# Scoring two neighbouring blocks of queries in one go, with one pool of four score and turn banks

## The reference

```python
# first block: 8 heads of 64; causal, ALiBi slope (with 2 blocks of 256 and top-1 selection,
# every earlier key is attended)
s = q.k * 64**-0.5 - slope * (tq - ks);  s = where(ks <= tq, s, -1e30)
out = softmax(s) @ v
# second block, layer 0: differential attention, 8 heads, two score matrices per head, all 512 keys
pr = softmax(s);  a = pr[:, 0] - lam * pr[:, 1];  o = rms_norm(a @ v) * 0.8
# second block, layer 1: sliding window, 16 query heads on 4 key/value heads, |i-j| <= 128, and a
# sink logit per head, which takes part in the softmax but has no value
mask = abs(kpos - qpos) <= 128
m = max(max(s), sink);  e = exp(s - m);  pr = e / (sum(e) + exp(sink - m))
```

## Time and profile before

| | us |
|---|---|
| median of 3 runs (lowest, highest) | 1973.62 (1973.46, 1975.21) |
| span of the profiled execution | 1972.9 |
| first attention, about | 36 to 166 |
| differential attention, about | 730 to 955 |
| sliding attention, about | 1385 to 1545 |

### The profile page before, as it was taken

One profiled execution on the slowest core, in us unless ns is written; L12 is line 12 of the kernel. 1 busy time (PEld: TensorE's weight loads), 2 busy tenths in 40 slices (PEclk: granted clock), 3 DMA queues, 4 the chain that ended last, 5 costly groups with the idle time before them and its releaser, 6 DMA issues.

```text
span 1972.9 us, 25163 instructions
## 1 busy us (share of the span) xinstructions
PE 1940.0 (98%) x9232; PEld 1590.0 (81%) x9232; DVE 1188.4 (60%) x1952; ACT 924.4 (47%) x1740; POOL 1109.2 (56%) x842
## 2 busy tenths in 40 slices
PE   8999999999999999999999999999999999999997
PEld 6877888888888877777888888888777888888886
DVE  6773325353433488877675646856688675746855
ACT  5653336533333366555453433445477543443443
POOL 5345544454444456454576665755785576666662
PEclk9999999999999999999999999999999999999998
DMA  4122233232232321111322222223110323222321
GB/s 160 65 70 96 89 114 128 95 104 102 97 111 94 111 98 68 45 65 54 128 103 100 97 96 97 97 90 109 65 54 33 128 97 107 97 86 96 107 93 57
DMA packets 52106, 182.72 MB, mean 93 GB/s; under 512 B 5776, under 2 KB 6160, under 8 KB 51984
## 3 DMA queue, kind: packets, MB, share of 16 engines
q1 hardware_dynamic: 51984, 181.12, 26.4%
HBM read 174.80 MB, written 6.29 MB: 92 GB/s over the span
## 4 chain that ended last, share of the span: by engine, by line
PE 92%; DVE 5%; ACT 1%; issue 1%; DMA 0%; POOL 0%; SPq 0%; DVEq 0%; ACTq 0%; POOLq 0%
PE b L393 28%; PE b L395 28%; PE b L394 28%; PE b L415 2%; PE b L407 1%; PE b L448 1%; PE b L439 1%; PE b L438 1%; DVE sm L574 1%; PE b L408 1%; PE b L409 1%; DVE ra L621 1%; DVE fa L586 0%; PE b L426 0%; DVE ra L483 0%
## 5 line engine op out<-in xcount | busy, mean ns | idle before, releaser
L239 POOL TENSOR_TENSOR ra<-raw,ra 128x512 fp32r<-128x512 f32 x632 | 883.2, 1405 | 771.7 <-ACT ra L283 770.0
L393 PE MATMUL b<-ra 128*128 128x512 f32 x2528 | 1000.7, 396 | 15.9 <-POOL ra L239 9.4
L395 PE MATMUL b<-ra 128*128 128x512 f32 x2528 | 985.9, 390 | 0.0
L394 PE MATMUL b<-ra 128*128 128x512 f32 x2528 | 985.2, 390 | 0.0
L283 ACT ACTIVATE ra<-raw 128x512 fp32r<-128x512 f32 x632 | 392.8, 628 | 531.9 <-PE b L395 526.4
L393 PEld LDWEIGHTS b<-ra 128*128 128x128 f32 x2528 | 475.5, 188 | 121.2 <-issue 15.2
L395 PEld LDWEIGHTS b<-ra 128*128 128x128 f32 x2528 | 475.0, 188 | 101.0
L394 PEld LDWEIGHTS b<-ra 128*128 128x128 f32 x2528 | 475.7, 188 | 93.3
L737 DVE TENSOR_TENSOR h<-b,h 128x512 f32<-128x512 f32 x136 | 91.8, 683 | 61.4 <-PE b L395 60.6
L628 DVE TENSOR_TENSOR tmp<-b,rb 128x512 f32<-128x512 f32 x62 | 42.4, 689 | 100.2 <-PE b L395 100.0
L621 DVE TENSOR_TENSOR ra<-b,ra 128x512 fp32r<-128x512 f32 (+4 forms) x166 | 91.9, 567 | 17.6 <-ACT ra L334 14.8
(11 more groups left out here) (276 smaller groups left out, 1900.4 us busy)
## 6 DMA issues: line engine op xcount, KB each, us to landing
raw<-in_f_g SPq DMA_DIRECT2D x40, 512.0 KB, 3.5
raw<-in_f_v SPq DMA_DIRECT2D x40, 512.0 KB, 3.5
raw<-in_f_d SPq DMA_DIRECT2D x40, 512.0 KB, 3.5
raw<-in_w_up SPq DMA_DIRECT2D x32, 512.0 KB, 3.5
raw<-in_w_down SPq DMA_DIRECT2D x32, 512.0 KB, 3.5
raw<-in_p_g SPq DMA_DIRECT2D x16, 512.0 KB, 3.5
raw<-in_w_gp SPq DMA_DIRECT2D x8, 512.0 KB, 3.4
raw<-in_w_ga SPq DMA_DIRECT2D x8, 512.0 KB, 3.4
```

The costliest lines, as they stand in the source:

```text
L239: e.tensor_tensor(wl, src, wh.bitcast(F), ALU.subtract).then_inc(*w_low.mark(n))
L393: e.matmul(ps, wh[:, c:c + 128], xh, start=start, stop=False)
L394: e.matmul(ps, wh[:, c:c + 128], xl, start=False, stop=False)
L395: last = e.matmul(ps, wl[:, c:c + 128], xh, start=False, stop=stop)
```

## The change

Two neighbouring blocks of queries, i and i + 1, are scored in one step of the planner. That step issues four tiles (12 matmuls) where there were two steps of two tiles, and it needs four free banks and four free probability buffers (in the differential attention two buffers of each kind). The two pairs of banks become one pool of four, QB, from which scores and turns take the bank that comes free first. With the banks no longer tied to heads, the sink column is written for every tile, after its score and before its `mask_min`: 64 copies. The planner's duration of a score step changes with it.

```diff
-            return (3 * (0.012 + a[1] / 2400.0) + 0.2) if a[4] == 0 else 0.04
+            return (3 * (0.012 + a[1] / 2400.0) + (0.35 if a[10] else 0.0)) if a[4] == 0 else 0.02
...
-    sbk = [2, 3]
-    tbk = [4, 5]
+    QB = [2, 3, 4, 5]
...
+    def picked(n):
+        ready = sorted((b for b in QB if bank_free[b] is not None), key=lambda b: sc.time_of(bank_free[b]))
+        return ready[:n] if len(ready) >= n else None
+    def pick(l):
+        ready = [b for b in l if bank_free[b] is not None]
+        return min(ready, key=lambda b: sc.time_of(bank_free[b])) if ready else None
...
@@ turns_of, and in the same way v_tile @@
-                b = rot(tbk)
+                b = pick(QB)
...
@@ attention_pairs, soft @@
+            if sinks:
+                made += sinks(t, b, score)
             n = row("mask_min", x["p"][:, 0:wide], banks[b][:, c0(i):c0(i) + wide], mk, slope(t), nm, score,
                     (*x["free"], *made))
             v = done("ve", "soft_v", n)
             bank_free[b] = (v,)
-            if i == 3 and sinks and t + 2 < 2 * npairs:
-                sinks(t + 2, b)
...
@@ attention_pairs, scores; together is 2 in both calls @@
-            for i in range(4):
+            for i2 in range(0, 4, together):
                 def need():
-                    if len(PB.free) < 2 or None in (bank_free[sbk[0]], bank_free[sbk[1]]):
+                    if len(PB.free) < 2 * together or picked(2 * together) is None:
                         return None
...
-                yield 8 * p + 2 * i, "pe", need
+                yield 8 * p + 2 * i2, "pe", need
+                steps = []
+                for i in range(i2, i2 + together):
+                    for t in (2 * p, 2 * p + 1):
+                        b = pick(QB)
+                        n = row("score", b, nk, c0(i), (qh, ql), rw, (kh, kl), i, lo, bank_free[b], (*qt, *kt_), i == i2)
+                        steps.append((t, i, b, done("pe", "score", n)))
+                for x in steps:
+                    launch(soft(*x))
...
@@ attention_diff, scores @@
-                    if not PB.free or not T.free or None in (bank_free[sbk[0]], bank_free[sbk[1]]):
+                    if len(PB.free) < 2 or len(T.free) < 2 or None in [bank_free[b] for b in QB]:
...
-        def sinks(t, b):
-            sunk[t] = (done("ve", "soft_v", row("sink_column", b, t, bank_free[b])),)
-            bank_free[b] = sunk[t]
+        def sinks(t, b, score):
+            return (done("ve", "soft_v", row("sink_column", b, t, (score,))),)
```

More of the change, by code:

```diff
@@ L401, in tensor_program @@
         elif kind == "score":
-            b, nk, c0, (qh, ql), row, (kh, kl), i, lo, free, ready = a
+            b, nk, c0, (qh, ql), row, (kh, kl), i, lo, free, ready, _ = a
             for t in free + ready:
@@ L1258, in need @@
                 def need():
-                    if (t, i) not in p_done or bank_free[tbk[0]] is None or (t and (t - 1, i // 2) not in used):
+                    if (t, i) not in p_done or pick(QB) is None or (t and (t - 1, i // 2) not in used):
                         return None
-                    return (p_done[(t, i)], *bank_free[tbk[0]])
+                    return (p_done[(t, i)], *bank_free[pick(QB)])
                 yield rank0(t) + per * i, "pe", need
@@ L1304, in heads, with attention_pairs @@
         launch(products_of(0))
-    def attention_pairs(npairs, Q, KT, VT, span, c0, sinks, mask_of, slope, O, PTb, norm_on):
+    def attention_pairs(npairs, Q, KT, VT, span, c0, sinks, mask_of, slope, O, PTb, norm_on, together):
         PB = Pool([fa[:, i, :] for i in range(8)])
@@ L1342, in need @@
                         return None
-                    return (*bank_free[sbk[0]], *bank_free[sbk[1]], *Q(2 * p)[3], *KT(2 * p)[3])
-                yield 8 * p + 2 * i, "pe", need
[L1345 to L1361, removed]
+                    return (*[t for b in picked(2 * together) for t in bank_free[b]], *Q(2 * p)[3], *KT(2 * p)[3])
+                yield 8 * p + 2 * i2, "pe", need
+                steps = []
+                for i in range(i2, i2 + together):
+                    lo, hi = span(i)
+                    nk = hi - lo
+                    for t in (2 * p, 2 * p + 1):
+                        k, buf, free = PB.get()
+                        nm, su = (sm[:, 24 + 4 * k + z:25 + 4 * k + z] for z in range(2))
+                        b = pick(QB)
+                        qh, ql, rw, qt = Q(t)
+                        kh, kl, krow, kt_ = KT(t)
+                        assert rw == krow
+                        n = row("score", b, nk, c0(i), (qh, ql), rw, (kh, kl), i, lo, bank_free[b], (*qt, *kt_), i == i2)
+                        bank_free[b] = None
+                        wide = mask_of(t, i)[0].shape[-1]
+                        tile[(t, i)] = dict(k=k, p=buf, free=free, nm=nm, su=su, wide=wide, nb=nk // 128)
+                        steps.append((t, i, b, done("pe", "score", n)))
+                for x in steps:
+                    launch(soft(*x))
             scored.add(p)
@@ L1406, in scores @@
         def scores(t):
-            for i in range(4):
+            for i2 in (0, 2):
                 def need():
-                    if not PB.free or not T.free or None in (bank_free[sbk[0]], bank_free[sbk[1]]):
+                    if len(PB.free) < 2 or len(T.free) < 2 or None in [bank_free[b] for b in QB]:
                         return None
@@ L1412, in need @@
                         return None
[L1413 to L1429, removed]
+                    return (*[x for b in QB for x in bank_free[b]], *Q(t)[3], *KT(t)[3])
+                yield 8 * t + 2 * i2, "pe", need
+                steps = []
+                for i in (i2, i2 + 1):
+                    lo, hi = span(i)
+                    k, a, free = PB.get()
+                    ti, pb, tfree = T.get()
+                    bs, score = [], []
+                    for c in range(2):
+                        b = pick(QB)
+                        qh, ql, _, qt = Q(t)
+                        kh, kl, _, kt_ = KT(t)
+                        r = row("score", b, hi - lo, 0, (qh, ql), 64 * c, (kh, kl), i, lo, bank_free[b], (*qt, *kt_),
+                                i == i2)
+                        bank_free[b] = None
+                        bs.append(b)
+                        score.append(done("pe", "score", r))
+                    tile[(t, i)] = dict(k=k, p=a, free=free, ti=ti, pb=pb, pb_free=tfree,
+                                        su=(sum1(t, i), sm[:, 26 + 4 * k:27 + 4 * k]))
+                    steps.append((t, i, bs, score))
+                for x in steps:
+                    launch(soft(*x))
             scored.add(t)
@@ L1448, in process @@
             i, z, v = yield from scaled(x, b, tok, 5)
-            yield 0, "pe", lambda: (v, *bank_free[tbk[0]]) if gate() and bank_free[tbk[0]] is not None else None
-            tb = rot(tbk)
+            yield 0, "pe", lambda: (v, *bank_free[pick(QB)]) if gate() and pick(QB) is not None else None
+            tb = pick(QB)
             t = done("pe", "turned", row("turn", tb, z, 4, bank_free[tb], (v,)))
@@ L1640, in first_block @@
         attention_pairs(4, Q1, K1, V1, lambda i: (0, 128 * (i + 1)), lambda i: 0, None,
-                        lambda t, i: (m.mask[:, 384 - 128 * i:512], (t_cst,)), lambda t: 2.0 ** -(t + 1), O1, PT1, "v")
+                        lambda t, i: (m.mask[:, 384 - 128 * i:512], (t_cst,)), lambda t: 2.0 ** -(t + 1), O1, PT1, "v", 2)
         evac_first = (v_tile(u, VV, ("v", 0), always), qk_tile(0, 0, qs(0)), qk_tile(0, 1, None), pool_in(0))
@@ L2104, in second_block_sliding @@
         attention_pairs(8, Q3, K3, V3, lambda i: (max(0, 128 * i - 128), min(S, 128 * i + 256)),
-                        lambda i: (128, 0, 0, 128)[i], sinks, mask_of, lambda t: 0.125, O1, PT3, "p")
+                        lambda i: (128, 0, 0, 128)[i], sinks, mask_of, lambda t: 0.125, O1, PT3, "p", 2)
         evac_first = [v_tile(u, VV + g, ("v3", g), always) for g in range(2)]
```

3 lines of the change are left out of this document (1 added, 2 removed).

## The result

The changed kernel takes 2008.86 us (median of 4 runs, 2003.12 to 2010.13) against 1974.41 us for the kernel before on the same chip (4 runs, 1973.46 to 1975.50). The ratio is 1.0168, 95% interval 1.0155 to 1.018. The forecast was 1964.6 us, with a range from 1957 to 1977.

What follows compares the result with a forecast made beforehand. PE's queue was taken to set the end nearly everywhere, with DVE close in the late sliding attention. Terms: -15.2 + 4.5 + 1.4 + 0.5 = -8.8, about -9 from 1973.6, giving 1964.6 us; range 1957 to 1977.

Steps and rivals of the forecast that it cites:

- Part 3: Pool of four banks: waits mostly covered by linear steps; 1.4 us lost in the differential attention, 0.5 in the first.
- Part 1: Fewer entries into and exits from scores on PE: 40 x 0.38 = 15.2 us saved, inner border free.
- Part 4: The rest: planner's border price, DMA, ACT and POOL work, and choice of the bank free first, all taken as 0.
- The sign that the prediction itself had named: PE's idle time growing in the differential attention would show the forecast wrong, pointing to banks.
- Part 2: 48 more sink copies on DVE at 0.20 to 0.25 us: 4.5 of the sliding attention's 6.1 us gain given back.
- The second one, banks as the new bound: Scores wait for four free banks while turns take single ones, linear steps used up early: +6, 1980 us; chance 0.12.
- The third rival: The second two tiles of a score step run after the first two, three more spacings: +7, 1981 us; chance 0.05.

Runs made afterwards that it cites:

- Run 5: Changed kernel with the sliding attention's probability buffers cut to the tiles' widths, twelve in the same memory instead of eight: 1982.5 us, +7.8 against the kernel before.
- Run 9: Kernel before with six probability buffers instead of eight in the sliding attention, nothing else changed: 2005.6 us, +31.7.
- run 1: Changed kernel, but the sliding attention scores one block of queries per step; pool of four and copies per tile stay: 1976.1 us, +1.9 against the kernel before.
- run 3: Changed kernel without the sink logit: no sink copies, mask step one column narrower: 1987.0 us, +12.8 against the kernel before.
- run 8: Pool of four banks alone: changed kernel with every attention scoring one block per step, sink copies for every tile: 1981.4 us, +6.6 against the kernel before.
- run 2: Kernel before with the sink column copied for every tile between score and mask step, 64 copies instead of 16: 1994.8 us, +20.6.
- run 11: Kernel before with 64 extra one-column copies on DVE in the sliding attention that wait for nothing and nothing waits on: 1981.9 us, +8.1.
- run 7: Changed kernel with the sliding attention wholly as in the kernel before; the other two attentions keep joined steps: 1972.7 us, -2.1 against the kernel before.
- run 12: As run 7, with the sliding attention's buffers cut to twelve: 1972.4 us, -1.5 against the kernel before.
- run 4: Changed kernel, but sliding-attention turns are held back once a four-tile step has its buffers, q and k, until it issues: 1996.7 us, +22.5 against the kernel before.
- run 6: Changed kernel with both twelve sliding-attention buffers and no sink logit: 1977.7 us, +3.0 against the kernel before.

## Why the prediction was wrong

**The step that failed is Part 3**, the pool of four banks: "Where a `need()` is late by the planner's clock, a linear step is taken instead. Such steps run out at the end of an attention only, and there I count 1 us." In the sliding attention PE waits from the third pair on, and its waits add up to 20.9 us more than before (17.4, and 3.5 behind score steps). The clock, which the prediction had put at nothing ("so no term here is a clock term"), adds about 12.1. I worked out the time that banks are in use and left out the other condition of the same `need()`, four free buffers of eight. Eight tiles are a pair, so with steps of four only two steps fit. The next waits for turns, and the turns then take the banks. Run 5 shows 26.7 us of 34.5 for the buffers. Run 9 shows that a shortage of buffers is enough of a cause by itself. In the changed kernel it is one of three things that work together. To take away the steps of four tiles gives 32.6 us back (run 1), to take away the shortage of buffers 26.7, and to take away the copies 21.7 (run 3), which is more than twice the loss.

**Part 1 was right at the step and too large for the stage.** The trace has 40 runs of 12 matmuls, and inside them there is no cost at the inner border: L409 to L407 is 0.23, like L408 to L409 beside it, and the one 0.33 stands after the first L407. PE's timeline at a joined step of the differential attention:

```profile
733.96 0.39 PE L395 MATMUL b<-ra 128*128 128x512 f32 x1
734.28 0.50 PE L407 MATMUL b<-ra 64*128 64x512 f32 x2
734.61 0.40 PE L408 MATMUL b<-ra 64*128 64x512 f32 x2
734.85 0.40 PE L409 MATMUL b<-ra 64*128 64x512 f32 x2
735.08 0.40 PE L407 MATMUL b<-ra 64*128 64x512 f32 x2
735.32 0.39 PE L408 MATMUL b<-ra 64*128 64x512 f32 x2
735.54 0.40 PE L409 MATMUL b<-ra 64*128 64x512 f32 x2
735.87 0.50 PE L393 MATMUL b<-ra 128*128 128x512 f32 x1
```

Entry, second matmul and exit cost what the prediction read, and one of each is gone per joined step. But the differential stage, with PE's waits left out, is only 3.8 us shorter than before, where 6.1 was the forecast, and the first attention 2.15 where 3.0 was. That run 8 and run 1 differ by 6.0 us there is a coincidence, since 3.8 of it are waits. One part of the missing 2.3 us can be read in the trace: in the changed kernel 32 turns follow a linear matmul in this stage, where 11 did before, and they start 0.29 us after it where 0.23 is due. The rest is not shown. The waits with the pool take 1.2 to 2.3 us more, where Part 3 had counted 0.4 and Part 4 nothing. The sign that the prediction itself had named for this stands in the lines above: from 730 to 955 PE is idle for 5.1 us, and 3.1 before.

**Part 2 was mis-sized and named the wrong payer.** It gave 4.5 us of the sliding attention's gain back for the copies, and with steps of four tiles they cost 21.7 (run 3). A copy in the chain costs DVE 0.29 us in the lines of run 2, where the range was 0.20 to 0.25. DVE's time was not the point: from 1466 to 1510 DVE is busy 72% of the time, where over 95% had been forecast and 92% stood before. A loose copy costs 0.13 us (run 11), one in the chain with two fixed banks 0.43 (run 2). There are 64 of them as forecast:

```profile
L608 DVE COPY b<-sm 128x1 f32<-128x1 f32 x64 | 10.0, 157 | 2.8 <-PE b L409 2.6
```

**The rivals.** The second one, banks as the new bound, had the direction and the alternation of scores and turns, 18 us per pair where 19.7 were measured on average. It had a chance of 0.12 and 1980 us. What it lacked is the buffers, which start the alternation, and the clock, which adds 12.1 us in the sliding attention. The third rival (the second pair does not overlap) is excluded by the timeline above, where all four tiles are ready. Something like it appears where a bank is late in the middle of a step:

```profile
1489.03 0.29 PE L409 MATMUL b<-ra 64*128 64x256 f32 x2
1490.05 0.44 PE L407 MATMUL b<-ra 64*128 64x384 f32 x1 [0.73 <-DVE ra L621]
1490.33 0.33 PE L408 MATMUL b<-ra 64*128 64x384 f32 x1
1490.38 0.44 PE L407 MATMUL b<-ra 64*128 64x384 f32 x1
1490.50 0.34 PE L409 MATMUL b<-ra 64*128 64x384 f32 x1
```

The third tile of the step waits 0.7 us for its bank and the fourth starts 0.33 later. These two still pass each other. Seven of the 16 steps of the sliding attention are broken up in this way, and in four of them the fourth tile starts only when the third is through. The undisturbed steps take 1.1 us each, and the seven take 10.7 us more than that together, 3.5 of them in the turn behind. That is why the score steps take more time than before with half of the borders.

**What stays open.** Why the pool (or the planner's new price) brings 5.0 us of waits into the differential attention with steps of two tiles, what the rest of Part 1's gain went into, what the four banks that must be free together cost by themselves, and which of bank time and DVE's order makes the copies of run 2 so dear.

## What to carry to other kernels

Before a producer's step is doubled, count every resource that the step must find free at once, against the pool: where two doubled steps fill it, the pipeline runs in phases, and the work that covered its waits is used up early. A saving at the busiest engine, even one priced to 0.1 us, holds only while the chain beside it keeps its pace, and a test with a slightly smaller pool in the old kernel (run 9) shows how near to that edge it stands. A tiny instruction that others wait for is to be priced by its wait, not by its duration. When the difference of two runs agrees with a forecast, it is worth splitting into waits and work once more: here most of the agreement was waits (run 8).

## What the runs showed of the hardware

**The clock falls in some executions after a wait of PE and not in others.** The program is the same up to the sliding attention in run 1 and run 7. In both, PE waits for about 1.9 us, up to 136.08 in run 7 and 135.18 in run 1. In run 7 the matmuls behind the wait then come to start 0.43 us apart where 0.23 is usual, which is the lower of the two levels:

```profile
136.08 0.47 PE L393 MATMUL b<-ra 128*128 128x512 f32 x1 [1.92 <-DVE tmp L628]
136.39 0.40 PE L394 MATMUL b<-ra 128*128 128x512 f32 x1
136.62 0.55 PE L395 MATMUL b<-ra 128*128 128x512 f32 x1
136.97 0.63 PE L393 MATMUL b<-ra 128*128 128x512 f32 x1
137.39 0.63 PE L394 MATMUL b<-ra 128*128 128x512 f32 x1
137.82 0.63 PE L395 MATMUL b<-ra 128*128 128x512 f32 x1
```

The granted clock from 121 to 149 is 0.94 in run 7 and 1.00 in run 1, and the first attention's stage takes 302.2 us against 300.6. So one wait can cost its own length and another 1.6 us. Eight traces here share this program up to the sliding attention, all with this wait of 1.9 us. The clock fell behind it in five (the changed kernel and runs 3, 5, 7 and 12) and not in three (runs 1, 4 and 6). In the five with the program of the kernel before, the wait there is 1.0 us, and it fell in none. In the changed kernel's sliding attention, with waits of up to 2.6 us, it comes to about 12.1 us.

**Matmuls on different rows of the array (0 to 63 and 64 to 127) overlap across twelve in a row**, with no cost between the first six and the next six: the first L409 and the second L407 start 0.23 us apart (734.85 to 735.08). The second matmul of a step still comes 0.10 us late, at 0.33 (734.28 to 734.61), and so does the one behind the step (735.54 to 735.87).
